# Low parts of the query weights on GpSimd, a reordered top-k selection, and three other moves around it

## The reference, cut to what matters

```python
h = h + peer(hn, peer_query, peer_sub_keys, peer_down, peer_up)
return rms_norm(h, final_norm_gain)
```

## Time and profile before

| | us |
|---|---|
| median of 3 runs (2944.47 to 2950.55) | 2948.95 |
| profiled execution, device time | 2950.64 |
| its span | 2948.8 |
| busy in the span: PE, PEld | 2814.4, 2303.8 |
| busy in the span: DVE, ACT, POOL | 2062.5, 1118.8, 539.3 |
| granted TensorE clock, mean | 0.985 |

### The profile page before, as it was taken

How to read it: one execution, slowest core, us unless ns; L and a number is a source line. 1 busy time by engine, 2 the same in 40 slices (tenths; PEclk the granted TensorE clock), 3 DMA queues, 4 the chain that set the end, 5 groups by cost and what they waited for, 6 DMA issues and landing times.

```text
span 2948.8 us, 41367 instructions
## 1 busy us (share of the span) xinstructions
PE 2814.4 (95%) x16385; PEld 2303.8 (78%) x16385; DVE 2062.5 (70%) x3111; ACT 1118.8 (38%) x1741; POOL 539.3 (18%) x534
## 2 busy tenths in 40 slices
PE   6899999999999999999999999999999889999997
PEld 4699999997879988798997798888878777444443
DVE  5687777778775456754655668985568999666666
ACT  3344444445454444544455542012117986000000
POOL 1000000000000000000000002333445457544443
PEclk9999999999999999999999999999999999999999
DMA  9977777777866644365443546999998888999997
GB/s 386 351 261 265 265 267 263 267 266 252 299 207 189 175 124 156 127 200 176 136 123 128 198 140 234 349 331 391 403 366 282 291 295 317 407 409 409 409 410 319
DMA packets 345760, 799.60 MB, mean 271 GB/s; under 512 B 40104, under 2 KB 95648, under 8 KB 344800
## 3 DMA queue, kind: packets, MB, share of 16 engines
q1 hardware_dynamic: 270576, 505.70, 49.6%
q0 software_dynamic: 74992, 291.27, 26.3%
HBM read 794.76 MB, written 2.10 MB: 270 GB/s over the span
## 4 chain that ended last, share of the span: by engine, by line
PE 53%; DMA 22%; DVE 13%; ACT 5%; issue 4%; POOL 3%; SPq 0%; DVEq 0%; ACTq 0%; POOLq 0%
PE ps L2019 16%; PE ps L2021 15%; PE ps L2020 15%; DMA s<-in_up_rows,s 12%; DMA s<-in_down_rows,s 8%; DVE s L1953 4%; POOL s L719 3%; DVE s L1972 2%; ACT s L1163 1%; DMA s<-in_ada_first 1%; DVE r L1246 1%; DMA s<-in_ret_first 1%; ACT r L734 1%; PE ps L2313 1%; ACT s L1133 1%
## 5 line engine op out<-in xcount | busy, mean ns | idle before, releaser
L2019 PE MATMUL ps<-r,r 128*128 128x256 f32 (+1 forms) x3232 | 1043.8, 323 | 9.9 <-DVE r L1246 7.6
L2021 PE MATMUL ps<-r,r 128*128 128x256 f32 (+1 forms) x3232 | 1024.2, 317 | 0.0
L2020 PE MATMUL ps<-r,r 128*128 128x256 f32 (+1 forms) x3232 | 1024.1, 317 | 0.0
L1246 DVE TENSOR_TENSOR r<-s,r 128x1024 fp32r<-128x1024 f32 (+2 forms) x532 | 640.3, 1212 | 413.1 <-ACT r L734 412.1
L734 ACT CAST r<-s 128x1024 fp32r<-128x1024 f32 (+2 forms) x532 | 550.0, 1041 | 766.7 <-PE ps L2021 708.2
L2019 PEld LDWEIGHTS ps<-r,r 128*128 128x128 f32 x3232 | 618.3, 191 | 67.0 <-issue 19.9
L2020 PEld LDWEIGHTS ps<-r,r 128*128 128x128 f32 x3232 | 618.6, 191 | 43.1 <-issue 5.3
L2021 PEld LDWEIGHTS ps<-r,r 128*128 128x128 f32 x3232 | 618.0, 191 | 40.2
L2703 PE MATMUL ps<-s,big 128*128 128x512 f32 x1024 | 441.8, 594 | 2.0 <-DMA s<-in_up_blocks 2.0
L1972 DVE SCALAR_TENSOR_TENSOR s<-s,s,s 128x1024 f32<-128x1024 f32 x256 | 329.2, 1286 | 162.9 <-DMA s<-in_up_rows,s 155.6
L1953 DVE CUSTOM_DVE_ANT_0 s<-s,s 128x1152 f32<-128x1152 f32 x256 | 345.8, 1353 | 111.2 <-DMA s<-in_down_rows,s 110.9
(11 more groups left out here) (314 smaller groups left out, 2240.4 us busy)
## 6 DMA issues: line engine op xcount, KB each, us to landing
s<-in_ada_w SPq DMA_DIRECT2D x128, 512.0 KB, 5.4
s<-in_up_blocks SPq DMA_DIRECT2D x128, 512.0 KB
s<-in_ret_w_in SPq DMA_DIRECT2D x112, 512.0 KB, 5.5
s<-in_down_blocks SPq DMA_DIRECT2D x128, 448.0 KB
s<-in_w_in SPq DMA_DIRECT2D x96, 512.0 KB, 3.9
s<-in_ada_first SPq DMA_DIRECT2D x64, 512.0 KB, 7.9
s<-in_ret_w_out SPq DMA_DIRECT2D x64, 512.0 KB, 5.6
s<-in_ret_w_in SPq DMA_DIRECT2D x112, 256.0 KB, 3.8
```

Of the source, the lines that this page charges most:

```text
L1246: v.tensor_tensor(lo_of(w), raw_of(w), hi_of(w).bitcast(F), ALU.subtract).then_inc(*lo_made.to(w))
L2019: pe.matmul(o, lh, rh, start=start, stop=False, skip_group_check=True)
L2020: pe.matmul(o, lh, rl, start=False, stop=False, skip_group_check=True)
L2021: return pe.matmul(o, ll, rh, start=False, stop=stop, skip_group_check=True)
```

## The change

GpSimd makes the low parts of the last 22 query units, behind a signal of its own (`lo_pool`), before it begins with the rows; all that waited for `lo_made` waits for the signal that belongs to the unit. DVE makes the first 10 and then runs 148 selection steps without a pause, and three steps instead of four after each down row. The selection is cut in two: `best` makes the lists of 128 for one tile and one quarter of the key sets, `select` the rest; a second pair of tiles, VAL1 and IDX1, lets both tiles be listed before either is finished. The border of the first ring goes from row 56 to row 62. The first 32 picks stand behind rows 157 to 188 instead of 150 to 187. Four DMA signals become one, `d_late`, and the load of the gain row moves from SP, behind block 131, to GpSimd, behind its wait for the end of the build, ahead of row 326.

```diff
@@ -18,7 +18,7 @@
 G1C, G2C = D - D1, D - D2
 H2C = D2 // 2
 
-RINGS = ((0, 7), (56, 4), (256, 6), (320, 7))
+RINGS = ((0, 7), (62, 4), (256, 6), (320, 7))
 EARLY = RINGS[1][0]
 NS = 4
 EPS = 1e-6
@@ -265,6 +265,7 @@
         scratch, kept, kept2 = column(W), column(192 * KB + K_DM), column(192 * KB + K_PM)
         CA, EQ = scratch(4, 256)[0], scratch(64, 16)[0]
         VAL, IDX, IDF = scratch(16, 16)[0], scratch(16, 16)[0], scratch(16, 16)[0]
+        VAL1, IDX1 = scratch(8, 16)[0], scratch(8, 16)[0]
         TV, TC = scratch(8, 16)[0], scratch(128)[0]
         WK = scratch(256)[0]
         II = [scratch(128)[0] for _ in range(2)]
@@ -479,13 +480,18 @@
 
         d_first, d_cst, d_rows = dma_sig("d_first", range(2)), dma_sig("d_cst"), dma_sig("d_rows", range(1, 10))
         d_x, d_pos, d_dec, d_fb = (dma_sig(n) for n in ("d_x", "d_pos", "d_dec", "d_fb"))
-        d_fg, d_tab, d_ff, d_f2, d_step = (dma_sig(n) for n in ("d_fg", "d_tab", "d_ff", "d_f2", "d_step"))
+        d_late, d_step = dma_sig("d_late", ["fg", "tab", "ff", "f2"]), dma_sig("d_step")
         d_out = dma_sig("d_out", range(2))
         d_row = [dma_sig(f"d_row{i}", [n for n in range(512) if row_slot(n)[1] == i]) for i in range(7)]
         d_block = [dma_sig(f"d_block{i}", range(256 // NS)) for i in range(NS)]
 
         hi_made = sig("hi_made", range(NW))
-        lo_made = sig("lo_made", range(NW))
+        POOL_LO = range(PQW + 10, NW)
+        lo_made = sig("lo_made", [w for w in range(NW) if w not in POOL_LO])
+        lo_pool = sig("lo_pool", POOL_LO)
+
+        def lo_ready(w):
+            return (lo_pool if w in POOL_LO else lo_made).at(w)
         used_up = sig("used_up", range(NW))
 
 
@@ -638,7 +644,7 @@
 
         down_rows, up_rows, down_blocks, up_blocks = A["down_rows"], A["up_rows"], A["down_blocks"], A["up_blocks"]
 
-        PICK_AT = [150 + 6 * q // 5 for q in range(32)] + [189 + 2 * q for q in range(32)]
+        PICK_AT = [157 + q for q in range(32)] + [189 + 2 * q for q in range(32)]
         HOT_AT = [194 + 2 * q for q in range(29)] + [251, 252, 253]
 
 
@@ -652,7 +658,7 @@
                     if plan[o][0] == "mod":
                         sp.wait_ge(*(mod_t if plan[o][3][1] in TENSOR_K else ada_v).at(o))
                     elif plan[o][0] == "w":
-                        sp.wait_ge(*lo_made.at(w_of[o]))
+                        sp.wait_ge(*lo_ready(w_of[o]))
                     elif plan[o][0] == "ada":
                         sp.wait_ge(*ada_v.at(o))
                     else:
@@ -674,8 +680,6 @@
                     sp.wait_ge(*rows_used.at(255))
                 sp.dma_start(sbuf[b // 128][b % NS], down_blocks[b] if b < 128 else up_blocks[b - 128]).then_inc(
                     *d_block[b % NS].to(b // NS))
-                if b == 131:
-                    sp.dma_start(G16[0:16, :], A["final_norm_gain_2"].rearrange("(n p) -> n p", p=128)).then_inc(*d_f2.to("all"))
             for t in range(2):
                 sp.wait_ge(*last_made.at(t))
                 sp.dma_start(out[0][t * 128:(t + 1) * 128, :], X[:, t, :]).then_inc(*d_out.to(t))
@@ -698,12 +702,16 @@
             g.wait_ge(*gains.at(("N0", 1)))
             g.dma_start(flat(DTAB), A["decay"]).then_inc(*d_dec.to("all"))
             g.wait_ge(*rotated.at(("M", 3)))
-            g.dma_start(GBA, A["final_norm_g"].partition_broadcast(128)).then_inc(*d_fg.to("all"))
+            g.dma_start(GBA, A["final_norm_g"].partition_broadcast(128)).then_inc(*d_late.to("fg"))
             g.wait_ge(*fin_scaled.at((3, 1)))
-            g.dma_start(GBA[:, 0:896], A["table"][:, K_DM:K_END]).then_inc(*d_tab.to("all"))
+            g.dma_start(GBA[:, 0:896], A["table"][:, K_DM:K_END]).then_inc(*d_late.to("tab"))
             g.wait_ge(*att_out.at(("L", 15)))
-            g.dma_start(FFG, A["ffn_norm_gain_2"][0][D1:].partition_broadcast(128)).then_inc(*d_ff.to("all"))
+            g.dma_start(FFG, A["ffn_norm_gain_2"][0][D1:].partition_broadcast(128)).then_inc(*d_late.to("ff"))
             g.dma_start(STEPN, A["table"][:, K_STEP:K_ALL]).then_inc(*d_step.to("all"))
+
+            for w in POOL_LO:
+                g.wait_ge(*hi_made.at(w))
+                g.tensor_tensor(lo_of(w), raw_of(w), hi_of(w).bitcast(F), ALU.subtract).then_inc(*lo_pool.to(w))
 
             g.wait_ge(*query_copied.at((3, 1)))
             for n in range(512):
@@ -714,6 +722,7 @@
                     g.wait_ge(*gate_in.at(1))
                 if n == RINGS[3][0] + 6:
                     g.wait_ge(*built.at((1, 31)))
+                    g.dma_start(G16[0:16, :], A["final_norm_gain_2"].rearrange("(n p) -> n p", p=128)).then_inc(*d_late.to("f2"))
                 if before_row(n) >= 0:
                     g.wait_ge(*rows_used.at(before_row(n)))
                 g.indirect_dma_start(
@@ -1240,7 +1249,7 @@
                         first_products(i, *plan[i][3])
                     elif plan[i][0] == "ada":
                         ada(i, *plan[i][3])
-                    elif plan[i][0] == "w":
+                    elif plan[i][0] == "w" and w_of[i] not in POOL_LO:
                         w = w_of[i]
                         v.wait_ge(*hi_made.at(w))
                         v.tensor_tensor(lo_of(w), raw_of(w), hi_of(w).bitcast(F), ALU.subtract).then_inc(*lo_made.to(w))
@@ -1831,16 +1840,26 @@
                 v.max_index(idx[:, 8:16], val[:, 8:16], wk).then_inc(*steps.to())
                 yield
 
+            def tops(t, f):
+
+                a = slice(8 * f, 8 * f + 8)
+                return (VAL1, IDX1) if (t, f) == (1, 0) else (VAL[:, a, :], IDX[:, a, :])
+
+            def best(t, g):
+                val, idx = tops(t, g // 2)
+                v.wait_ge(*sel_copied.at((t, g)))
+                for j in range(4):
+                    hp, i = 4 * g + j, 4 * (g % 2) + j
+                    v.wait_ge(*steps.at())
+                    yield from top16(SC[t][:, hp * 128:(hp + 1) * 128], val[:, i, :], idx[:, i, :].bitcast(U32), WK[:, 0:128])
+
             def select(t, f):
-                for hp in range(8 * f, 8 * f + 8):
-                    if hp % 4 == 0:
-                        v.wait_ge(*sel_copied.at((t, hp // 4)))
-                    yield from top16(SC[t][:, hp * 128:(hp + 1) * 128], VAL[:, hp, :], IDX[:, hp, :].bitcast(U32), WK[:, 0:128])
-                    v.wait_ge(*steps.at())
                 a = slice(8 * f, 8 * f + 8)
-                V2 = VAL[:, a, :].rearrange("p (h a) k -> p h a k", a=2)
+                val, idx = tops(t, f)
+                V2 = val.rearrange("p (h a) k -> p h a k", a=2)
                 I2 = IDF[:, a, :].rearrange("p (h a) k -> p h a k", a=2)
-                v.tensor_copy(IDF[:, a, :], IDX[:, a, :].bitcast(U32)).then_inc(*steps.to())
+                v.wait_ge(*steps.at())
+                v.tensor_copy(IDF[:, a, :], idx.bitcast(U32)).then_inc(*steps.to())
                 yield
                 v.wait_ge(*steps.at())
                 v.tensor_tensor(CA.rearrange("p h (i j) -> p h i j", i=16),
@@ -1894,17 +1913,21 @@
                 v.wait_ge(*gate_made.at(t))
 
             def both():
-                for f in range(2):
+                for g in range(2):
                     for t in range(2):
-                        yield from select(t, f)
+                        yield from best(t, g)
+                for t in range(2):
+                    yield from select(t, 0)
+                for t in range(2):
+                    for g in (2, 3):
+                        yield from best(t, g)
+                    yield from select(t, 1)
 
             choice = both()
-            for g in range(4):
-                for u in range(8):
-                    step(PQW + 8 * g + u)
-                    if 8 * g + u >= 10:
-                        for _ in range(4):
-                            next(choice)
+            for u in range(10):
+                step(PQW + u)
+            for _ in range(148):
+                next(choice)
 
             def pick(t, q):
 
@@ -1947,7 +1970,7 @@
             for n in range(256):
                 t, j = n // 128, n % 128
                 if n:
-                    for _ in range(4):
+                    for _ in range(3):
                         next(choice, None)
                 v.wait_ge(*d_row[row_slot(n)[1]].at(n))
                 v.tensor_tensor_reduce(row_buf(n), row_buf(n), HNG[:, t, :], 1.0, 0.0, ALU.mult, ALU.add,
@@ -2022,7 +2045,7 @@
 
             def unit_T(w, u, last, bs, x, nk=2, ms=4, site=None):
 
-                pe.wait_ge(*lo_made.at(w))
+                pe.wait_ge(*lo_ready(w))
                 h, l = hi_of(w), lo_of(w)
                 for k in range(nk):
                     if site and (u * nk + k) % 2 == 0:
@@ -2691,7 +2714,7 @@
                 build_(1, q)
             for b in range(4, 8):
                 take(b)
-            pe.wait_ge(*d_f2.at("all"))
+            pe.wait_ge(*d_late.at("f2"))
             for n in range(16):
```

(6 more changed lines are left out.)

## The result

The changed kernel takes 2989.95 us (median of 4 runs, 2989.03 to 2992.42) against 2948.51 us for the kernel before in the same measurement: ratio 1.014, 95% interval 1.0126 to 1.0155. The forecast was 2981 with a range of 2969 to 3002.

What follows compares the result with a forecast made beforehand. Five stages, each with its own limit, TensorE and DMA full together in the last. -7.1 - 6.3 + 49.0 + 2.0 - 2.0 + 1.5 - 4.8 = +32.3 on 2950.64 gave 2982.9, less 1.7: 2981, range 2969 to 3002.

Steps and rivals of the forecast that it cites:

- rival (b): VectorE and GpSimd hinder each other during the two selections, selection ending 12 us later: 2989 us; chance 0.12.
- The gain row: Before the up products: GpSimd fetches it after up row 325 and TensorE's products wait: +49.0 us, bounds +45 and +56.
- clock term: Up products: TensorE, having stood for 50 us, may start at its lower clock level: +1.5 us.
- First up row: Row 256, needing row 254's buffer, is issued only 2 us before VectorE adds it: +2 us, bounds 0 and +4.
- The last stage: Up products to the end: block waits go (-2.0), lower clock (+1.5), final adds and squares sooner (-4.8).
- The tail: End of the products: tile 0's final adds start 3.4 us before the stream's end, squares already done: -4.8 us.
- First and second place: Projection to first pick: pick starts at ScalarE's copy, -7.1 us; first 32 picks: fewer row waits, -6.3 us.
- the second place: Pick 0 to pick 32: 73.3 us plus 1.2 us for waits, instead of 80.85: -6.3 us.
- Low parts on GpSimd: Query projection: a low part takes GpSimd no longer than TensorE's unit of 2.9 us, so cost 0.
- Rival (c): Projection: GpSimd is slower than a unit; at 4.0 us a low part TensorE waits 24 us: 3005; chance 0.06.

Runs made afterwards that it cites:

- e1: Changed kernel with the gain row's load back on SyncE behind up block 131: 2943.43 us, ratio 0.9978 to the kernel before.
- e2: Kernel before with only the gain row's load moved to GpSimd, ahead of row 326: 2995.10 us, ratio 1.0155.
- e3: Changed kernel with GpSimd still loading the gain row, but ahead of row 262 instead of 326: 2943.47 us, ratio 0.9981 to the kernel before.
- e4: As e1, with the border of the first ring at row 60 instead of 62: 2940.47 us, ratio 0.9975 to the kernel before.
- e7: As e4, but VectorE makes all 32 low parts and GpSimd none: 2951.81 us, ratio 1.0010 to the kernel before.
- e6: Kernel before with only the first 32 picks put behind rows 157 to 188: 2954.82 us, ratio 1.0025.
- e5: As e4, but the first 32 picks stand behind rows 150 to 187 again: 2947.59 us, ratio 1.0001 to the kernel before.
- e8: As e4, but the first 32 picks stand behind rows 160 to 188: 2942.43 us, ratio 0.9979 to the kernel before.

## Why the prediction was right

The direction and the main mechanism were right and the time lay in the range; it was 9 us low. Of these, 6.1 are in the terms (38.4 us measured between the profiled executions, 32.3 forecast); the rest is that I took 1.9 off for the median of before, while the median of the changed kernel lies 0.9 above its profiled execution. Three terms of the sum were mis-sized.

The price of rival (b), 2989, comes nearer to the measured time than the forecast does. That is luck: its mechanism cost 3.2 us of VectorE and nothing in the time, as shown below.

The bounds have two slips. The -19 for both places holds only the second (80.85 - 32 x 1.94 = 18.8); with the first pick's 7.1 it is -26. And rows at 1.28 us with a landing at once give +43 for the gain row, not +45. The lower end of the range should have been near 2960 instead of 2969, and the measured time lies inside either way.

**The gain row** (forecast +49.0, bounds +45 and +56; measured +57.1) is the step that decides, and e1, e2 and e3 show it as it was described: TensorE waits in front of all products for a load that GpSimd issues behind row 325, which waits for VectorE's adds. The 8.1 us between the sum and the row, and the 1.1 past its upper bound, come from three parts. (1) The 32 rows took 2518.27 - 2471.92 = 46.35 us, 1.45 each, instead of 44.0: some waited for their DMA. That is +2.3. (2) From issue to landing were 2528.26 - 2522.82 = 5.4 us and not the 3 that I took: +2.4. (3) The 16 gain matmuls ran at a granted clock of 0.50 and took 2535.35 - 2528.26 = 7.1 us instead of 3.9: +3.2. The forecast had its clock term only behind them, with the products. Between the end of row 319 and the issue lie 4.55 us, where the forecast had 4.4, but the path is another one. Row 323 did not go as soon as row 319 was done. GpSimd's last wait was the one before row 320, and from there six issues follow one another until the load goes at 2522.82:

```profile
2514.02 1.93 POOL L728 DMA_INDIRECT s<-in_up_rows,s  x1 [2.24 <-DVE s L1995]
```

These are 8.8 us of GpSimd's own issuing, so the load would not have gone much earlier had VectorE been faster with rows 317 to 319.

For (1), VectorE's up rows by line, from 2471.92 to 2518.3 (count, busy time and mean ns, idle time before them by what ended it):

```profile
L1995 DVE SCALAR_TENSOR_TENSOR s<-s,s,s 128x1024 f32<-128x1024 f32 x32 | 41.1, 1285 | 5.2 <-DMA s<-in_up_rows,s 2.3 <-DVE s L1995 0.5
```

The 2.3 us that a DMA ended are the whole difference to the pace of the earlier trace rows.

**First up row** (forecast +2, bounds 0 and +4; measured +3.95). The issue came 2.0 us before VectorE was ready, as forecast, and the landing took 6.0 us, the long end of the 4 to 6 named there. The row on GpSimd:

```profile
2408.41 1.81 POOL L728 DMA_INDIRECT s<-in_up_rows,s  x1 [8.28 <-DVE s L1976]
```

It is released by a down row's add, and 2408.41 + 5.98 is the add at 2414.39. The border at 60 takes the wait away (e4).

**The last stage.** For the products' -2.0 for waits and +1.5 for the clock, -1.3 was measured. The waits for blocks are gone (TensorE was busy 441.74 of the 443.7 us before, and all of 442.46 now), which is the -2.0; the busy time grew by 0.7. The first products, after and before, in two windows:

```profile
2535.40:2540.00 4.60, 4.60 (x7) 2.02 (x7) 4.18 (x5) 0.00 (x0) 3.69 (x4) 0.50 1.00 393
```

```profile
2487.90:2491.00 3.10, 3.10 (x5) 1.51 (x5) 2.68 (x3) 0.00 (x0) 2.38 (x2) 0.50 0.94 317
```

The stream begins at the lower clock in both kernels. In the changed one this lasts about 2.5 us longer, until nearly 2541. So the clock term was there, at half its size. The tail was -7.8 and not -4.8, for I had the wrong number of records. A product of 128x512 shows as two matmul records of some 0.43 us (1024 records are 512 products), so tile 0 is ready 16 records before the end, 6.9 us, and not 8. VectorE's first final add starts 7.7 us before the stream's end at 2977.81, having stood 64.42 us, as the up rows ended at about 2905.7:

```profile
2970.12 0.69 DVE L2011 TENSOR_TENSOR s<-ps,s 128x512 f32<-128x512 f32 x1 [64.42 <-PE ps L2726]
```

**First and second place** (forecast -7.1 and -6.3; measured -6.8 and -7.1) held, but the way to row 157 was not the one forecast, and the causes of the two places are tied together. Against the kernel before the ratios are:

| | old pick places | picks from row 157 |
|---|---|---|
| rows late | 1 | 1.0025 (e6) |
| rows early, border 60 | 1.0001 (e5) | 0.9975 (e4) |

Early rows alone gain nothing that can be told, later picks alone lose 0.25%, both together gain 0.25%. The forecast priced the two places as a pair, which was right; priced one by one, each edit would have been called useless. Row 157 was used at 2189.73 (forecast 2193), but two errors cancel in that. Row 0 was used at 1818.75, 7 us later than forecast: the part ahead of the change is 1.7 us late, GpSimd's neighbourhood costs 3.2 (below), and each of two selections takes 20.3 us undisturbed (e7) instead of 19.3. Row 58, used at 1959.79, was still 7 us late. From there the rows came every (2189.73 - 1959.79) / 99 = 2.32 us instead of 2.42, which gives 10 us back. That was luck: in e3 they came every 2.40. From row 157 to the first pick there were 9.5 us, not the 4 that I counted on, and VectorE stood for 7.9 of them (4.14 in the row above). In e3 there were 3.7, and it stood for 2.11:

```profile
2198.66 0.75 DVE L1946 SCALAR_TENSOR_TENSOR s<-ps,s,s 128x512 f32<-128x512 f32 x1 [2.11 <-issue]
```

So the reserve varies from execution to execution, and in e8 three rows more used it up in one at least. For the second place the forecast named only waits for rows. A part is the clock: 0.94 over the picks in the earlier trace rows, where TensorE had stopped for VectorE's late pick, 1.00 in the changed kernel. The stop in the kernel before:

```profile
2205.11 1.12 PE L2613 MATMUL ps<-r 128*128 128x128 f32 x4 [5.38 <-DVE s L1921]
```

e6, which has the new places and a clock of 0.73 at its start, needs 74.7 us for the picks, so the clock's part may be 1 us or a little more of the 7.1, an estimate from single executions.

**Low parts on GpSimd** (forecast 0). Rival (c) falls on its price:

```profile
L714 POOL TENSOR_TENSOR r<-s,r 128x1024 fp32r<-128x1024 f32 x22 | 54.4, 2474 | 104.0 <-ACT r L743 104.0
```

```profile
1784.25 2.42 POOL L714 TENSOR_TENSOR r<-s,r 128x1024 fp32r<-128x1024 f32 x1 [0.48 <-ACT r L743]
```

These are the page's group and one instance. The mean is 2.47 us, below the 2.9 of a unit. GpSimd itself waited for ScalarE (90.4 of the 104.0 us before its first low part), and TensorE was busy for all of the 68 us from 1726 to 1794 in which GpSimd made them. The estimate from the Trainium skill (GPSIMD Engine Reference, elementwise cycle accounting), 2.25 us, is 0.2 below the mean in the trace.

**Rival (b)** was there, and small. GpSimd and VectorE, around the second half of the first selection:

```profile
1788.02 2.57 POOL L714 TENSOR_TENSOR r<-s,r 128x1024 fp32r<-128x1024 f32 x1 [1.35 <-ACT r L743]
1790.90 3.03 POOL L714 TENSOR_TENSOR r<-s,r 128x1024 fp32r<-128x1024 f32 x1 [0.31 <-ACT r L743]
...
1787.12 1.23 DVE L1884 TENSOR_TENSOR s<-s,s 128x1024 f32<-128x1024 f32 x1
1788.38 3.29 DVE L1888 TENSOR_TENSOR s<-s 128x1024 f32<-128x1024 f32 x1
1791.70 1.22 DVE L1892 TENSOR_REDUCE s<-s 128x64 f32<-128x1024 f32 x1
1792.96 1.02 DVE L1881 CAST s<-s 128x64 f32<-128x64 uint32 x1
```

L1888 takes 1.22 us when GpSimd is idle. Here it starts at 1788.38, inside a low part that ends at 1790.59, and ends 1.1 us after that; the next low part starts beside it and takes 3.03 us instead of 2.40. That is how one would look that waits for the other whole instruction, as the Trainium skill states it (SBUF — State Buffer, Who interferes with whom). This trace agrees in this place. The CAST, at 1.02 us instead of 0.20, was stretched too, also beside a low part. e7 settles whose doing this is: it selects in the same order and makes no low part on GpSimd. Its two instructions, with line numbers two higher, take what they take alone:

```profile
1810.58 1.23 DVE L1890 TENSOR_TENSOR s<-s 128x1024 f32<-128x1024 f32 x1
...
1813.10 0.20 DVE L1883 CAST s<-s 128x64 f32<-128x64 uint32 x1
```

The five experiments that keep the low parts on GpSimd (e1, e3, e4, e5, e8) show 3.29 or 3.30 us and 1.02 us again. GpSimd's low parts are thus the cause. The price is small, as such instructions are few among the selection's steps and GpSimd's low parts end with the projection: the first selection takes 23.5 us (1774.70 to 1798.19) in the changed kernel and 20.3 (1797.21 to 1817.50) in e7, so 3.2 us of VectorE, where rival (b) had 12. Rows and the reserve before the first pick covered it.

## What to carry to other kernels

- A small load costs what stands in front of it in its queue. Before moving one, write down what the instructions ahead of it wait for, and what waits for it: here 8 KB behind row gathers held back 442 us of products, for 1.4% of the kernel, while the same load on the same engine 64 rows earlier was free.
- Two edits can each be worth nothing and together be worth a gain, when one makes data early and the other uses that it is early. Try them as a pair, and both alone, before dropping either.
- When a reserve of a few us stands ahead of a chain of TensorE and VectorE, leave it there. In e8's profiled execution the stop that came when it was used up lasted 3.82 us, and the lower clock behind it made the loss more than 10.

## What the runs showed that I had not expected

- After a stop of 3.82 us TensorE's granted clock was 0.50 from 2207 to 2223, although TensorE was busy all that time (e8), and 0.73 in the 25 us that hold most of a stop of 12.88 (e6). After 54.86 us it was 0.50 for the 16 gain matmuls and for the first products, and 1.00 from 2542 on.
- The gain row landed 5.4 us after its issue behind row gathers; a single up row's landing took 6.0. The one moves 8 KB and the other 512 KB, and these two landings hardly differ.
- Removing 52.8 us from the end of the products (e1) gave 45.9 us of span, since the final adds, free in the changed kernel, wait for the rows again.
